# Top-k selection shared by VectorE and GpSimd beside two attentions, and a second bank of scores per head for narrow tiles

## What is computed

```
score = einsum('bth,bths->bts', wi, relu(einsum('bthd,bsd->bths', qi, ki)))
score = where(admiss, score, NEG)
_, sel = top_k(score, 256)                  # equal scores: the lower position first
logits = (q . k[sel]) * HEAD_DIM ** -0.5 + bias
o = softmax(logits) @ v[sel]
```

## Time and profile before

| what | value |
|---|---|
| median of 3 runs | 1732.3 us (1729.9 to 1732.46) |
| the profiled execution's own time | 1729.48 us |
| its span in the trace | 1727.7 us |
| PE busy | 1540.9 us (89%) |
| DVE busy | 763.1 us (44%) |
| ACT busy | 635.7 us (37%) |
| POOL busy | 167.4 us (10%) |
| first attention (first pair masked on DVE to the barrier) | 451.4 to 614.9 us |
| second attention (first scores to the last GpSimd product) | 614.9 to 799.6 us |

### The profile page before, as it was taken

The page is one execution under the profiler, slowest core; times in us unless marked ns, Lnnn a source line. Parts: engine busy times, 40 slices in busy tenths (PEclk is TensorE's granted clock), DMA queues, the critical chain, the costliest instruction groups (busy, mean ns, idle before and its releaser), DMA issues. The chain is left out here.

```text
span 1727.7 us, 24006 instructions
## 1 busy us (share of the span) xinstructions
PE 1540.9 (89%) x9370; PEld 1287.8 (75%) x9370; DVE 763.1 (44%) x1501; ACT 635.7 (37%) x1254; POOL 167.4 (10%) x156
## 2 busy tenths in 40 slices
PE   2699799998688868986997999999999999999997
PEld 0476685688455535654785999999999998887876
DVE  2411238888677788643563111111111113455454
ACT  3210235576676546753443111111111112443432
POOL 2131110112000000001121000000000001011020
PEclk9899899999789969986998999999999999999999
DMA  9377310011301020004322111111111113644442
GB/s 310 142 268 238 87 32 24 19 44 31 139 14 40 20 45 20 14 7 143 112 85 68 49 43 42 49 49 37 48 49 49 40 45 121 226 135 133 149 143 90
DMA packets 116325, 146.80 MB, mean 85 GB/s; under 512 B 15616, under 2 KB 91728, under 8 KB 114160
## 3 DMA queue, kind: packets, MB, share of 16 engines
q1 hardware_dynamic: 114384, 140.70, 25.2%
q0 software_dynamic: 1856, 4.98, 0.9%
HBM read 128.61 MB, written 19.02 MB: 85 GB/s over the span
## 5 line engine op out<-in xcount | busy, mean ns | idle before, releaser
L1602 PE MATMUL ps<-h_hi,w_hi 128*128 128x352 f32 x1056 | 340.8, 323 | 4.7 <-DVE w_lo L1642 4.7
L1602 PE MATMUL ps<-h_lo,w_hi 128*128 128x352 f32 x1056 | 341.9, 324 | 0.0
L1602 PE MATMUL ps<-h_hi,w_lo 128*128 128x352 f32 x1056 | 341.6, 323 | 0.0
L1602 PEld LDWEIGHTS ps<-h_hi,w_hi 128*128 128x128 f32 x1056 | 199.2, 189 | 4.8 <-DVE w_lo L1642 4.8
L1602 PEld LDWEIGHTS ps<-h_hi,w_lo 128*128 128x128 f32 x1056 | 199.2, 189 | 0.0
L1602 PEld LDWEIGHTS ps<-h_lo,w_hi 128*128 128x128 f32 x1056 | 199.1, 189 | 0.0
L1642 DVE TENSOR_TENSOR w_lo<-raw_weights,w_hi 128x1024 fp32r<-128x1024 f32 x44 | 53.7, 1222 | 235.9 <-ACT w_hi L1616 235.9
L909 PE MATMUL ps<-h_hi,wb_hi 128*128 128x352 f32 x384 | 128.1, 334 | 20.2 <-ACT queries L798 9.6
L1740 PE MATMUL ps<-w_hi,a_hi 128*128 128x512 f32 x352 | 137.7, 391 | 3.9 <-DVE a_lo L1552 3.7
L1740 PE MATMUL ps<-w_hi,a_lo 128*128 128x512 f32 x352 | 137.0, 389 | 0.0
L1740 PE MATMUL ps<-w_lo,a_hi 128*128 128x512 f32 x352 | 137.0, 389 | 0.0
(11 more groups left out here) (221 smaller groups left out, 2688.8 us busy)
## 6 DMA issues: line engine op xcount, KB each, us to landing
front_work<-in_w_ada SPq DMA_DIRECT2D x24, 1024.0 KB, 7.0
raw_more<-in_w_down SPq DMA_DIRECT2D x34, 512.0 KB, 3.4
raw_weights<-in_w_down SPq DMA_DIRECT2D x32, 512.0 KB, 3.2
raw_weights<-in_w_gate SPq DMA_DIRECT2D x22, 512.0 KB, 3.7
raw_weights<-in_w_up SPq DMA_DIRECT2D x22, 512.0 KB, 3.8
w_raw<-in_w_in SPq DMA_DIRECT2D x32, 256.0 KB, 2.9
values_keys<-in_x_prompt SPq DMA_DIRECT2D x4, 1024.0 KB, 17.0
attention_work<-scratch_rinv SPq DMA_DIRECT2D x32, 128.0 KB, 3.1
```

The source lines that it names most:

```text
L1602: mm = nc.tensor.matmul(B(3 * i + c, CH), cut[i][a][:, P * k:P * k + P], h[:, NTOK * k + CH * c:NTOK * k + CH * (c + 1)], start=(k == 0 an ...
```

## The change

1. **Selection is divided.** A tile now takes three background steps instead of six: part 0 (the complement `not_sure` is marked, and `need` is computed there), part 1 (the candidates, now by a product), part 2 (the running sum). The other three operations go to GpSimd as four instructions in `finish_selection(t)`. A fixed table, `SELECT_AFTER`, says before which tile's normalising product GpSimd runs them: tiles 2 and 3 before the product of tile 5 of the first attention, 4, 5 and 6 before those of tiles 6, 7 and 8, and tiles 7 and 8 before the products of tiles 0 and 1 of the second.
2. **Waits.** `scanned` holds GpSimd until VectorE's running sum of the tile. `selected` counts GpSimd's four instructions a tile; VectorE's part 0 of tile t waits for tile t - 2, its part 1 for tile t - 1 (three buffers are shared in turn), and the masks of the second attention for their tile.
3. **Fewer background steps.** The first attention runs 37 of them (s = 0 to 36), the second the last six (s = 0 to 5).
4. **Two banks a head.** A pair with at most 512 keys needs one bank a head; pairs with even and odd numbers now alternate between the head's two banks, and their scores wait for pair s - 2 instead of s - 1.

```diff
-    return ("bisect", x // 3, x % 3) if x <= 3 * BISECTIONS else ("select", 2 + (x - 3 * BISECTIONS - 1) // 6, (x - 3 * BISECTIONS - 1) % 6)
+    return ("bisect", x // 3, x % 3) if x <= 3 * BISECTIONS else ("select", 2 + (x - 3 * BISECTIONS - 1) // 3, (x - 3 * BISECTIONS - 1) % 3)
...
         if part == 0:
-            link(nc.vector.tensor_scalar(sure, x, T(R_HI + t - 2, 1, r), 0.0, ALU.is_gt, ALU.add, accum_out=T(R_NSURE, 1, r)))
+            if t >= 4:
+                dve.wait_ge(ctx.selected, 4 * (t - 3))
+            link(nc.vector.tensor_scalar(not_sure, x, T(R_HI + t - 2, 1, r), 0.0, ALU.is_le, ALU.add, accum_out=T(R_NSURE, 1, r)))
+            link(nc.vector.tensor_scalar(need, T(R_NSURE, 1, r), 1.0, float(TOPK - w), ALU.mult, ALU.add))
         elif part == 1:
-            nc.vector.tensor_scalar(need, T(R_NSURE, 1, r), -1.0, float(TOPK), ALU.mult, ALU.add).then_inc(bis, 1)
-            links[0] += 1
-            link(nc.vector.scalar_tensor_tensor(cand, x, T(R_LO + t - 2, 1, r), sure, ALU.is_ge, ALU.subtract))
+            if t >= 3:
+                dve.wait_ge(ctx.selected, 4 * (t - 2))
+            link(nc.vector.scalar_tensor_tensor(cand, x, T(R_LO + t - 2, 1, r), not_sure, ALU.is_ge, ALU.mult))
         elif part == 2:
-            link(nc.vector.tensor_tensor_scan(x, cand, cand, 0.0, ALU.add, ALU.max))
-        elif part == 3:
-            link(nc.vector.scalar_tensor_tensor(cand, x, need, cand, ALU.is_le, ALU.mult))
-        elif part == 4:
-            link(nc.vector.tensor_tensor(sure, sure, cand, ALU.add))
-        elif part == 5:
-            link(nc.vector.tensor_scalar(x, sure, -BIG, BIG, ALU.mult, ALU.add))
+            nc.vector.tensor_tensor_scan(x, cand, cand, 0.0, ALU.add, ALU.max).then_inc(ctx.scanned, 1)
...
+SELECT_AFTER = (((), (), (), (), (), (2, 3), (4,), (5,), (6,)), ((7,), (8,), (), (), (), (), (), (), ()))
...
-    LAST_X = 3 * BISECTIONS + 6 * (NT - 2)
+    BACKGROUND = len(PAIRS) + 1 if band else steps
+    LAST_X = 3 * BISECTIONS + 3 * (NT - 2)
...
+    def narrow(s):
+
+        return width(PAIRS[s][0]) <= 512
+
+    def score_bank(u):
+
+        return 2 * (u % 2) + (u // 2 % 2 if narrow(u // 2) else 0)
...
+                pool.wait_ge(ctx.scanned, t - 1)
+                nc.gpsimd.tensor_scalar(x, x, T(R_NEED + t, 1, r), None, ALU.is_le).then_inc(ctx.selected, 1)
+                pool.wait_ge(ctx.selected, 4 * t - 7)
+                nc.gpsimd.tensor_tensor(cand, x, cand, ALU.mult).then_inc(ctx.selected, 1)
+                pool.wait_ge(ctx.selected, 4 * t - 6)
+                nc.gpsimd.tensor_tensor(x, not_sure, cand, ALU.subtract).then_inc(ctx.selected, 1)
+                pool.wait_ge(ctx.selected, 4 * t - 5)
+                nc.gpsimd.tensor_scalar(x, x, BIG, None, ALU.mult).then_inc(ctx.selected, 1)
+
             for t in range(NT):
+                for t2 in SELECT_AFTER[0 if band else 1][t]:
+                    finish_selection(t2)
...
-                    if s:
-                        pe.wait_ge(masked, 2 * s)
+                    free = 2 * s - 2 if narrow(s) else 2 * s
+                    if free > 0:
+                        pe.wait_ge(masked, free)
...
-                if x0 + s <= LAST_X:
+                if s < BACKGROUND and x0 + s <= LAST_X:
                     step(x0 + s)
```

More of the change, by code:

```diff
@@ L639, in background_step, with select_buffers @@
 def background_step(x):
-    return ("bisect", x // 3, x % 3) if x <= 3 * BISECTIONS else ("select", 2 + (x - 3 * BISECTIONS - 1) // 6, (x - 3 * BISECTIONS - 1) % 6)
+    return ("bisect", x // 3, x % 3) if x <= 3 * BISECTIONS else ("select", 2 + (x - 3 * BISECTIONS - 1) // 3, (x - 3 * BISECTIONS - 1) % 3)
+def select_buffers(t):
+    return [SCR[0], SCR[1], COUNT_JUNK][2 * t % 3], [SCR[0], SCR[1], COUNT_JUNK][(2 * t + 1) % 3]
 def searcher(nc, dve, T, ctx):
@@ L685, in select @@
         r, w = rows_of(t), width_b(t)
[L686 to L687 removed]
+        open_at, cand_at = select_buffers(t)
+        x, not_sure, cand = T(score_at(t), w, r), T(open_at, w, r), T(cand_at, w, r)
+        need = T(R_NEED + t, 1, r)
         if part == 0:
[L689 removed]
+            if t >= 4:
+                dve.wait_ge(ctx.selected, 4 * (t - 3))
+            link(nc.vector.tensor_scalar(not_sure, x, T(R_HI + t - 2, 1, r), 0.0, ALU.is_le, ALU.add, accum_out=T(R_NSURE, 1, r)))
+            link(nc.vector.tensor_scalar(need, T(R_NSURE, 1, r), 1.0, float(TOPK - w), ALU.mult, ALU.add))
         elif part == 1:
[L691 to L693 removed]
+            if t >= 3:
+                dve.wait_ge(ctx.selected, 4 * (t - 2))
+            link(nc.vector.scalar_tensor_tensor(cand, x, T(R_LO + t - 2, 1, r), not_sure, ALU.is_ge, ALU.mult))
         elif part == 2:
[L695 to L701 removed]
+            nc.vector.tensor_tensor_scan(x, cand, cand, 0.0, ALU.add, ALU.max).then_inc(ctx.scanned, 1)
     def step(x):
@@ L731, in project @@
     ctx.bis, ctx.mid_ready, ctx.counted = sem("bis"), sem("mid_ready"), sem("counted")
+    ctx.scanned, ctx.selected = sem("scanned"), sem("selected")
     ctx.links = [0]
@@ L1079, in _, with finish_selection @@
                     nc.gpsimd.memset(T3(BIAS_A, HEADS, 640)[64:128, lo:hi, 0:64], BIG).then_inc(edge_done, 1)
+            def finish_selection(t):
+                r, w = rows_of(t), width_b(t)
+                open_at, cand_at = select_buffers(t)
+                x, not_sure, cand = T(score_at(t), w, r), T(open_at, w, r), T(cand_at, w, r)
+                pool.wait_ge(ctx.scanned, t - 1)
[6 more added lines that the diff above has]
+                nc.gpsimd.tensor_scalar(x, x, BIG, None, ALU.mult).then_inc(ctx.selected, 1)
             for t in range(NT):
+                for t2 in SELECT_AFTER[0 if band else 1][t]:
+                    finish_selection(t2)
                 r = rows_of(t)
@@ L1119, in _ @@
                         for i in range(2):
-                            mm = nc.tensor.matmul(B(2 * i + lo // 512, hi - lo, r), T(q_at + NTOK * c + P * t, r, HD, HD * i),
+                            mm = nc.tensor.matmul(B(score_bank(2 * s + i) + lo // 512, hi - lo, r), T(q_at + NTOK * c + P * t, r, HD, HD * i),
                                                   key_source(t, c, i, lo, hi), start=True, stop=True)
@@ L1250, in _ @@
                         for u in (2 * s, 2 * s + 1):
-                            ready = add_bias(u, B(2 * (u % 2), main - near, r, c0=near), near, main)
+                            ready = add_bias(u, B(score_bank(u), main - near, r, c0=near), near, main)
                     for u in (2 * s, 2 * s + 1):
@@ L1261, in _ @@
                             dve.wait_ge(part, ready)
+                            if t >= 2:
+                                dve.wait_ge(ctx.selected, 4 * (t - 1))
                             other = T(R_M01 + P * (1 - t), w) if t < 2 else T(score_at(t), main, r)
@@ L1279, in _ @@
                         read_item(dve, "v", first[s] + j)
-                if x0 + s <= LAST_X:
+                if s < BACKGROUND and x0 + s <= LAST_X:
                     step(x0 + s)
-    ctx.searched = x0 + steps
+    ctx.searched = x0 + BACKGROUND
 def load_gu(sp, ins, raw, i, f):
```

4 lines of the change are left out of this document (1 added, 3 removed).

## The result

The changed kernel took **1738.88 us** (median of 9 runs, 1734.43 to 1741.44) against 1731.62 us of the kernel before, measured in the same rounds (9 runs, 1726.29 to 1732.46): a ratio of 1.0043, 95% interval 1.0032 to 1.0054. It is slower, by 7.3 us, and lies above the forecast's range. The profiled execution took 1738.94 us, with a span of 1737.1 us.

What follows compares the result with a forecast made beforehand. VectorE's selection was held to be on the path in steps 0 to 19 of the second attention. Terms -0.5, +1.6, +0.65, 0, -2.8 and -1.65 gave -2.7 us: 1729.6 from 1732.3, range 1724.4 to 1736.0.

Steps and rivals of the forecast that it cites:

- GpSimd's chain becomes the bound: Rival, chance 0.15: the barrier after tile 6 and part 1 of tile 8 wait for GpSimd's chain; slower, 1738.0 us.
- a low clock in steps 8 to 11: Second attention, in the slower rival: TensorE's clock stays low throughout, 3.7 us more than the 2.3 already charged.
- The price of the one-tensor instructions: GpSimd's two instructions with one tensor: 1.3 us each at 1024 columns, 1.15 at 896, high end 2.38.
- a sign of being wrong: GpSimd's one-tensor instructions above 2 us or below 0.8 would show the prediction wrong.
- The two-tensor price: GpSimd's two instructions with two tensors: 2.38 us each at 1024 columns, 2.1 at 896.
- The stall in step 4: Second attention: VectorE's part 1 of tile 8 waits for GpSimd's tile 7, 3.7 us (3.0 to 5.8).
- The end of the first attention: GpSimd's product becomes last, at 613.9 us, after 6.8 us for tile 6; VectorE had ended at 614.4 before.
- The race: Second attention, end of GpSimd's tile 7: VectorE's part 1 of tile 8 and GpSimd's first product start together; 0.65 us charged.
- Contention elsewhere at nothing: Apart from the one race, VectorE and GpSimd holding each other up was costed at nothing.
- Steps 8 to 19: Second attention: steps 8 to 11 gain 0, steps 12 to 15 gain 2.8 us, steps 16 to 19 gain 1.65.
- The first attention's narrow tiles: Scores could be issued a step early, but TensorE comes late for another reason: 0.7 us gained (0 to 2).
- The second bank buys nothing: Rival, chance 0.18: a ring bank or `leave` holds TensorE's in-order list before the scores everywhere; 1733.1 us.

Runs made afterwards that it cites:

- Number 8: Changed kernel with tile 8's VectorE parts moved to steps 11 to 13 and its GpSimd chain before the product of tile 2: 1729.73 us, ratio 0.9987 to before.
- number 1: Kernel before with only the second bank of scores added, whole selection on VectorE: 1731.48 us, ratio 0.9996.
- number 5: Kernel before with the second bank and all six selection parts still on VectorE, packed where it is idle: 1724.01 us, ratio 0.9946.
- 6: Kernel before with all six selection parts packed where VectorE is idle, without the second bank: 1729.54 us, ratio 0.9982.
- number 7: Changed kernel with VectorE's parts of tiles 6 to 8 and GpSimd's chains of tiles 5 to 8 placed later: 1718.52 us, ratio 0.9912 to before.
- 9: Changed kernel with selection parts and GpSimd's chains placed later, as in number 7, but one bank a head: 1723.47 us, ratio 0.9963 to before.
- number 10: Changed kernel with GpSimd's last instruction a product of two tensors, the second a repeated column: 1735.71 us, ratio 1.0015 to before.
- number 3: Changed kernel with GpSimd's four instructions on half of each tile's columns, so masks are wrong: 1726.32 us, ratio 0.9972 to before.

## Why the prediction was wrong

The mechanism that won was among the rivals, "GpSimd's chain becomes the bound", at 1738.0 us, and with 0.15 it was given too little. That its number lies so near 1738.88 is partly luck: it charged 3.7 us for a low clock in steps 8 to 11, where 0.6 more than forecast came, and had nothing for a wait that cost 2.7. Two steps of the working failed: a price, and a wait that was left out. The price alone adds 5.5 us at the two places (2.6 and 2.9), an estimate from the chains' lengths; 1729.6 and that is 1735.1, still inside the range. It took the second to leave it. Point by point:

- **The price of the one-tensor instructions: the first step that failed.** I took 1.3 us at 1024 columns and 2.38 as the upper bound. They measured 2.85 (the comparison) and 2.77 (the product), beyond the bound and past the 2 us that the prediction named as a sign of being wrong, and more than the two-tensor ones beside them. My reason for that bound, that one tensor can't cost more than two, was an assumption and no row. The two-tensor price was right (2.35 for 2.38; 2.07 for 2.1 at 896 columns). Tile 7 so took 10.6 us instead of 7.7 (7.0 to 9.8), tile 6 9.4 instead of 6.8. The Trainium skill ("GPSIMD Engine Reference", 4.1 Engine selection) calls one-input work on GpSimd roughly line-rate; here it took over twice VectorE's 1.28 us for the same shape, and the measurement decides.
- **The stall in step 4: right place, wrong size.** It stood before part 1 of tile 8 and was ended by line 1107, as written, and the running sum of tile 7 ended 8.8 us after the first scores where 8.6 was forecast. It lasted 6.55 us instead of 3.7 (3.0 to 5.8); the chain's 2.9 us explain the difference. Number 8 took it away, with what stood around it, and gained 9.7.
- **The end of the first attention, the second step that failed: forecast 0.2 us later from step 35 on, measured 5.5.** The chain's extra 2.6 us is one half. The other is a wait that I put at nothing: part 1 of tile 6 waits for GpSimd's tile 5, which takes 8.2 us (601.26 to 609.49). That is 2.71 us, and 1.1 more for the lost race; the rest of that stretch was 1.1 us shorter than I had counted. I had written the running sum of tile 6 down by its step number alone, and asked what waits for GpSimd only at tile 8.
- **The race: right kind, other place.** It was charged at tile 7 in the second attention, where GpSimd's product in fact came 12.7 us later, waiting for its transfer. It was lost in the last step of the first attention, at 2.26 us for 1.15.
- **Contention elsewhere at nothing: right but for one place.** Part 1 of tile 5, at 595.16 in the first attention, took 2.13 us beside GpSimd's product from 595.21, where such an operation on 768 columns takes 1.03. What that cost in time no run separates; steps 16 to 35 as a whole took 0.6 us more than before. VectorE's other selection instructions kept their durations (running sum of tile 7 2.29 for 2.21, part 1 of tile 7 1.28, as in the earlier trace rows).
- **Steps 8 to 19: right.** Steps 12 to 15 took 12.5 us for a forecast of 12.7, steps 16 to 19 16.84 for 16.8. Steps 8 to 11 began at the low clock, as charged, and cost 15.05 for 14.5.
- **The first attention's narrow tiles: right in steps 0 to 8, open behind.** The 0.7 us came, in steps 0 to 8. Steps 8 to 35 were put at 0 and cost 2.0 more in the trace; 1.4 of that is in steps 8 to 16, with a lower clock, and not clear of what kernels with the same instructions differ by.
- **"The second bank buys nothing"** was a rival too, and number 1 alone would bear it out. Numbers 5 and 6, and 7 and 9, show that it does buy something once nothing else holds VectorE.

## What to carry to other kernels

Moving work to an idle engine turns busy time into latency: here 13.7 us of VectorE became 54.5 us of GpSimd, in chains of 4.7 to 11 us, growing with the tile. Before such a move, list for every moved piece who waits for its end (buffers shared in turn and barriers too) and put at least the chain's length of other work between; the same instructions gave 1.0043 or 0.9912 by placement alone. Bound the price of an operation from the far side by something measured on that engine in that form: "fewer operands, so no dearer" is not a bound.

## What the hardware showed

- **GpSimd is slower with one tensor and a scalar than with two tensors.** At 128x1024 in float32: comparison with a per-row scalar 2.85 us, product with a constant 2.77, product or difference of two tensors 2.35, and product with a repeated column 1.89. On 32 rows and 1056 columns they take 2.95, 2.88 and 2.43: the rows are free, the columns count.
- **VectorE with two SBUF inputs and GpSimd exclude each other for whole instructions.** 2.26 us for 1.15 on VectorE in the change, 2.16 for 1.27 on GpSimd in number 10. The Trainium skill ("SBUF — State Buffer", Who interferes with whom) says that the shared ports are an exclusive lock held for the whole instruction and that the order of issue decides who blocks; the traces agree on the lock. On the order they agree where the recorded starts lie apart: in the kernel before and in numbers 1, 5 to 7, 9 and 10, whenever VectorE's start led by 0.12 us or more it kept its own duration, and where GpSimd's led by 0.28 to 0.56 VectorE was the longer one (1.45 us for 0.61 in number 5, 2.02 for 1.30 in number 8). Where VectorE's recorded start led by only 0.04 or 0.05 us, both occur: it lost with part 1 in the change, and in number 3 its running sum kept its 2.02 us while GpSimd's product took 3.06 for 1.27.
- **What follows a stall of TensorE is not set by its length.** Behind a stall of 6.37 us in front of step 7 steps 8 to 11 took 15.05 us, behind one of 1.64 (number 3) 15.5, and in number 8, where TensorE had worked without a gap before step 8, 11.42. In the first two the four matmuls of step 8 took 1.65 us, in the third 0.92: the granted clock was 0.50 before the stall already, and what parts the three is whether it had risen by step 8.
- **The second bank goes with a lower clock in steps 8 to 16 of the first attention.** In the eight kernels that have it the granted clock there is 0.76 to 0.86 and the stretch 36.2 to 38.7 us, in the four without it 0.82 to 0.95 and 33.6 to 37.3. The groups overlap, and within each the instructions of this stretch are the same. That is a comparison of single executions, and no run took the bank from the first attention alone; so whether number 7 would gain by that is open.
